# Branch A's up-projections, regrouped: head pairs of unrotated rows, one rotation product for four heads

## The reference

```python
def mla_mixer(xq, xkv, q_norm_g, w_q_up, kv_norm_g, w_kv_up):
    cq = rmsnorm(xq, q_norm_g)
    q = (cq @ w_q_up).reshape(b, s, H_A, DA_NOPE + DA_ROPE)
    q = jnp.concatenate([q[..., :DA_NOPE], rope(q[..., DA_NOPE:], pos)], axis=-1) * (DA_NOPE + DA_ROPE) ** -0.5
    ckv = rmsnorm(xkv[..., :KV_LORA], kv_norm_g)
    k_rope = rope(xkv[..., None, KV_LORA:], pos)
    kv = (ckv @ w_kv_up).reshape(b, s, H_A, DA_NOPE + DA_V)
    k = jnp.concatenate([kv[..., :DA_NOPE], jnp.broadcast_to(k_rope, (b, s, H_A, DA_ROPE))], axis=-1)
    v = kv[..., DA_NOPE:]
    ...
```

## Time and profile before

| | |
|---|---|
| median of 3 runs | 3025.38 us (3019.72 to 3032.05) |
| span of the profiled execution | 3027.5 us (the page gives no other time of it) |
| PE busy | 2832.9 us, 94% of the span |
| DVE busy | 2117.6 us, 70% |
| ACT busy | 1651.9 us, 55% |
| PE clock, mean granted | 0.972 of 2.4 GHz |
| `upA` in layer 0 | 98.24 to 127.56 us of the span |
| `upA` in layer 1 | 1590.07 to about 1619.4 us |

### The profile page before, as it was taken

One profiled execution on the slowest core, in us unless ns is written; L12 is line 12 of the kernel. 1 busy time (PEld: TensorE's weight loads), 2 busy tenths in 40 slices (PEclk: granted clock), 3 DMA queues, 4 the chain that ended last, 5 costly groups with the idle time before them and its releaser, 6 DMA issues. The chain is left out here.

```text
span 3027.5 us, 44165 instructions
## 1 busy us (share of the span) xinstructions
PE 2832.9 (94%) x14520; PEld 2263.1 (75%) x14520; DVE 2117.6 (70%) x3015; ACT 1651.9 (55%) x2612; POOL 690.0 (23%) x563
## 2 busy tenths in 40 slices
PE   5999999899899999999779999989998999999995
PEld 4677776677678888888666777866776888888884
DVE  5544456555589899999845444565546989999997
ACT  2342433432358788888534434244323778888883
POOL 0100000000145653333200000001001567533330
PEclk9999999999999999999889999999998999999997
DMA  7224342233569999999812243422334999999995
GB/s 234 79 75 148 118 134 96 74 120 133 208 239 359 354 364 373 366 373 364 309 57 80 87 153 111 153 70 90 124 120 189 349 355 353 364 381 368 369 353 228
DMA packets 124560, 671.52 MB, mean 222 GB/s; under 512 B 27628, under 2 KB 29036, under 8 KB 90444
## 3 DMA queue, kind: packets, MB, share of 16 engines
q1 hardware_dynamic: 91040, 605.91, 54.4%
q0 software_dynamic: 31424, 57.44, 5.7%
q10 hardware_dynamic: 1932, 6.16, 0.9%
HBM read 656.60 MB, written 55.28 MB: 235 GB/s over the span
## 5 line engine op out<-in xcount | busy, mean ns | idle before, releaser
L2158 DVE TENSOR_TENSOR ew_lo<-ew,e_hi 128x2048 fp32r<-128x2048 f32 x258 | 591.3, 2292 | 95.2 <-ACT e_hi L1954 95.2
L711 PE MATMUL bank<-h_hi,w_hi 128*128 128x512 f32 x1248 | 511.9, 410 | 35.1 <-DVE w_lo L645 16.5
L1954 ACT ACTIVATE e_hi<-ew 128x2048 fp32r<-128x2048 f32 x260 | 498.6, 1918 | 15.2 <-PE bank L2373 9.3
L711 PE MATMUL bank<-h_hi,w_lo 128*128 128x512 f32 x1248 | 504.3, 404 | 0.0
L711 PE MATMUL bank<-h_lo,w_hi 128*128 128x512 f32 x1248 | 502.0, 402 | 0.0
L645 DVE TENSOR_TENSOR w_lo<-raw,w_hi 128x1024 fp32r<-128x1024 f32 x198 | 242.1, 1223 | 301.1 <-ACT w_hi L637 300.6
L2373 PE MATMUL bank<-e_hi,x_hi 128*128 128x512 f32 x1040 | 418.2, 402 | 0.1
L2373 PE MATMUL bank<-ew_lo,x_hi 128*128 128x512 f32 x1040 | 408.5, 393 | 0.0
L2373 PE MATMUL bank<-e_hi,x_lo 128*128 128x512 f32 x1040 | 406.0, 390 | 0.0
L711 PEld LDWEIGHTS bank<-h_hi,w_hi 128*128 128x128 f32 x1248 | 240.1, 192 | 116.6 <-issue 44.2
L1842 POOL DMA_INDIRECT y_d<-y,idx x130 | 214.5, 1650 | 467.6 <-issue 401.0
(11 more groups left out here) (331 smaller groups left out, 5065.0 us busy)
## 6 DMA issues: line engine op xcount, KB each, us to landing
ew<-in_wexp SPq DMA_DIRECT2D x130, 2048.0 KB, 9.8
raw<-in_wmix SPq DMA_DIRECT2D x297, 512.0 KB, 3.5
ew<-in_wexp SPq DMA_DIRECT2D x130, 1024.0 KB, 10.2
ew<-y_d SPq DMA_DIRECT2D x8, 2048.0 KB, 11.7
ew<-y_d SPq DMA_DIRECT2D x8, 1024.0 KB, 7.8
ada0a<-in_ada SPq DMA_DIRECT2D x2, 2048.0 KB, 13.4
ada0b<-in_ada SPq DMA_DIRECT2D x2, 2048.0 KB, 22.2
h_d<-htok ACTq DMA_DIRECT2D x8, 512.0 KB, 10.8
```

The costliest lines, as they stand in the source:

```text
L711: ins = nc.tensor.matmul(out, lhs, rhs, start=start, stop=stop)
L1954: nc.scalar.activation(e_hi[h][:], up_part(ew, j, h), ACT.Copy).then_inc(whi_done, 1)
L2158: nc.vector.tensor_tensor(up_part(ew_lo, j, h), up_part(ew, j, h), e_hi[h][:].bitcast(F32), ALU.subtract).then_inc(wlo_done, 1)
```

## The change

It regroups `upA`. Keys: 4 jobs `knope` with two heads' 64 unrotated rows each, in place of 8. Queries: 4 jobs `qnope` with two heads' unrotated rows each and 2 jobs `qrope` with four heads' 32 rotated rows each, in place of 8 jobs of 96 rows. Values stay 4 jobs. The weights' columns are brought into that order when the tile is split (`split_parts`), since the tiles in memory stay as they were: the high and low parts are written through rearranged views. The queries go first, then key and value jobs in turn.

The copy out of a pair is two ACT instructions of 64 partitions, one for each head. The rotation is one fp32 product by a 128 x 128 matrix `turn4` for four heads, twice; DVE multiplies 128 rows twice and then adds 32 rows at a time, four times, from partitions 0, 32, 64, 96 into partitions 64 to 95 of `qA`. No rotation stands after `late`. POOL makes `turn4` from the identity at the layer's start (two operations), and SP loads the cosine and sine table four times, once for each 32 partitions.

```diff
-    j["upA"] = ([Job("T", [("kvup",)], "kA", act="ckv", k=1, col=P * h, arg=h) for h in range(HA)]
-                + [Job("VA", [("kvup",)], "vA", act="ckv", k=1, arg=t) for t in range(TC)]
-                + [Job("T", [("qup", h // 4)], "qA", act="cq", k=2, m=DQ, col=DQ * (h % 4), arg=h) for h in range(HA)])
+    j["upA"] = []
+    for t in range(2):
+        j["upA"] += [Job("T", [("qup", t)], "qrope", act="cq", k=2, col=4 * NOPE, arg=t)]
+        j["upA"] += [Job("T", [("qup", t)], "qnope", act="cq", k=2, col=P * i, arg=2 * t + i) for i in range(2)]
+    for i in range(TC):
+        j["upA"] += [Job("T", [("kvup",)], "knope", act="ckv", k=1, col=P * i, arg=i),
+                     Job("VA", [("kvup",)], "vA", act="ckv", k=1, arg=i)]
...
+        def split_parts(u, q):
+            kind = TILES[u][0]
+            src, hi, lo = raw[u % RAW][:], w_hi[q % SPLIT][:], w_lo[q % SPLIT][:]
+            if kind == "kvup":
+                src = src.rearrange("p (h a c) -> p h a c", a=2, h=HA)
+                hi, lo = [w.rearrange("p (a h c) -> p h a c", a=2, h=HA) for w in (hi, lo)]
+            if kind != "qup":
+                return [(hi, src, lo)]
+            src = src[:, 0:8 * DQ].rearrange("p (k h c) -> p k h c", k=2, h=4)
+            hi, lo = [w[:, 0:8 * DQ].rearrange("p (k c) -> p k c", k=2) for w in (hi, lo)]
+            parts = []
+            for c0, c1 in ((0, NOPE), (NOPE, DQ)):
+                h, l = [w[:, :, 4 * c0:4 * c1].rearrange("p k (h c) -> p k h c", h=4) for w in (hi, lo)]
+                parts.append((h, src[:, :, :, c0:c1], l))
+            return parts
...
-            nc.scalar.activation(w_hi[q % SPLIT][:], raw[u % RAW][:], ACT.Copy).then_inc(hi_done, 1)
+            for dst, src, _ in split_parts(u, q):
+                ins = nc.scalar.activation(dst, src, ACT.Copy)
+            ins.then_inc(hi_done, 1)
...
-            elif j.out == "kA":
-                nc.scalar.activation(kA[0:NOPE, j.arg, :], b[0:NOPE, :], ACT.Copy).then_inc(done, 1)
-            elif j.out == "qA":
-                nc.scalar.activation(qA[0:DQ, j.arg, :], b[0:DQ, :], ACT.Copy, scale=float(DQ) ** -0.5).then_inc(done, 1)
+            elif j.out in ("knope", "qnope"):
+                for i in range(2):
+                    dst = (kA if j.out == "knope" else qA)[0:NOPE, 2 * j.arg + i, :]
+                    ins = nc.scalar.activation(dst, b[NOPE * i:NOPE * i + NOPE, :], ACT.Copy,
+                                               scale=1.0 if j.out == "knope" else float(DQ) ** -0.5)
+                ins.then_inc(done, 1)
+            elif j.out == "qrope":
+                nc.scalar.activation(qrope[j.arg][:], b[:], ACT.Copy, scale=float(DQ) ** -0.5).then_inc(done, 1)
...
-                    sp.dma_start(rope_t[R, :, :], rope_d).then_inc(rope_in, 16)
+                    for i in range(4):
+                        sp.dma_start(rope_t[ROPE * i:ROPE * i + ROPE, :, :], rope_d).then_inc(rope_in, 16)
...
+                        nc.vector.tensor_tensor(qrot[:], MB[:], rope_t[:, 1, :], ALU.mult).then_inc(m_free, 1)
+                        link(dve, nc.vector.tensor_tensor(qrope[t][:], qrope[t][:], rope_t[:, 0, :], ALU.mult))
+                        for i in range(4):
+                            rows = slice(ROPE * i, ROPE * i + ROPE)
+                            nc.vector.tensor_tensor(qA[R, 4 * t + i, :], qrope[t][rows, :], qrot[rows, :], ALU.add
+                                                    ).then_inc(rot_ready, 1)
                     for j in jobs["upA"]:
                         dve_stream(dve, events_of([(j, 0, n_products(j))]))
-                        if j.out == "qA" and j.arg:
-                            rotate(j.arg - 1)
+                        if j.out == "qnope" and j.arg % 2 == 0:
+                            rotate(j.arg // 2)
                     dve_stream(dve, events_of(whole(jobs["late"])))
-                    rotate(HA - 1)
...
+                        nc.tensor.matmul(MB[:], turn4[:], qrope[t][:], start=True, stop=True).then_inc(m_full, 1)
```

More of the change, by code:

```diff
@@ L260, in hybrid_trunk @@
         lamv = place("lamv", [P, 256], at=m0 + 10240)
+        qrope = [place(f"qrope{i}", [P, S], at=m0 + 11264 + 2048 * i) for i in range(2)]
+        turn4 = place("turn4", [P, P], at=m0 + 15360)
+        assert t_end["turn4"] <= t_end["merged"]
         r0 = cursor[0]
@@ L382, in hybrid_trunk @@
         vecs_in, rope_in = sem("vecs_in"), sem("rope_in")
[L383 removed]
+        made_ready = sem("made_ready")
         amul_ready = sem("amul_ready")
@@ L581, in hybrid_trunk @@
         for key in ([("st", n) for n in ("x",)] + [("rb", "x"), ("rb", "cq"), ("rb", "ckv"), ("kr", 0)]
-                    + [("qr", h) for h in range(HA)] + [("ot", o) for o in range(16)] + [("st", "x2"), ("rb", "x2")]):
+                    + [("qr", t) for t in range(2)] + [("ot", o) for o in range(16)] + [("st", "x2"), ("rb", "x2")]):
             m_use[key] = len(m_use)
@@ L679, in make_products @@
                 for i, (w, a) in enumerate(parts):
-                    wv = W[w][:, 0, :].rearrange("p (h c) -> p h c", h=HA)[:, :, NOPE:]
-                    out.append((u, 0, A[a][:, 0, j.arg * P:(j.arg + 1) * P], wv, bank[:].rearrange("p (h c) -> p h c", h=HA),
+                    out.append((u, 0, A[a][:, 0, j.arg * P:(j.arg + 1) * P], W[w][:, 0, HA * NOPE:], bank[:],
                                 i == 0, i == 2))
@@ L724, in act_out @@
             done = chunk_out[j.c % 2]
-            if j.out not in ("cq", "ckv", "kA", "qA", "qB", "kB", "qC", "kC", "qD", "kD", "gate", "sg", "vt"):
+            if j.out not in ("cq", "ckv", "knope", "qnope", "qrope", "qB", "kB", "qC", "kC", "qD", "kD", "gate", "sg", "vt"):
                 return
@@ L1333, in _ @@
                     pool.wait_ge(pchain, 1)
-                    nc.gpsimd.memset(tabA[0:64, S - 64:S], NEG).then_inc(tabA_ready, 1)
+                    nc.gpsimd.memset(tabA[0:64, S - 64:S], NEG).then_inc(made_ready, 1)
+                    four = [P, 4, ROPE // 2]
+                    heads, eye = [a.rearrange("p (h c) -> p h c", h=4) for a in (turn4[:], ident)]
+                    nc.gpsimd.tensor_tensor(heads[:, :, 0:ROPE // 2], zero[:, 0:1].unsqueeze(2).broadcast_to(four),
+                                            eye[:, :, ROPE // 2:], ALU.subtract).then_inc(made_ready, 1)
+                    nc.gpsimd.tensor_copy(heads[:, :, ROPE // 2:], eye[:, :, 0:ROPE // 2]).then_inc(made_ready, 1)
                     load_table(0)
@@ L1492, in _, with rotate @@
                     nc.tensor.matmul(MB[R, :], prot, qraw[R, :], start=True, stop=True).then_inc(m_full, 1)
-                    def rotate(h):
-                        wait_out_of(pe, "qA", h)
-                        wait_mb_free(pe, ("qr", h))
-                        nc.tensor.matmul(MB[R, :], prot, qA[R, h, :], start=True, stop=True).then_inc(m_full, 1)
+                    def rotate(t):
+                        wait_out_of(pe, "qrope", t)
+                        pe.wait_ge(made_ready, 3)
+                        wait_mb_free(pe, ("qr", t))
+                        nc.tensor.matmul(MB[:], turn4[:], qrope[t][:], start=True, stop=True).then_inc(m_full, 1)
                     for j in jobs["upA"]:
                         pe_products(pe, j, 0, n_products(j))
-                        if j.out == "qA" and j.arg:
-                            rotate(j.arg - 1)
+                        if j.out == "qnope" and j.arg % 2 == 0:
+                            rotate(j.arg // 2)
                     products_of(jobs["late"])
-                    rotate(HA - 1)
                     for br in "ABCD":
```

22 lines of the change are left out of this document (10 added, 12 removed).

## The result

The changed kernel takes 3009.21 us (median of 4 runs, 3005.16 to 3012.63) where the kernel before, on the same chip, takes 3025.36 (4 runs): a ratio of 0.9941, 95% interval 0.9927 to 0.9954. So it is 16.2 us faster, inside the range of the prediction (2996 to 3014), but 6 us short of its 3003, and at the upper edge of the 2998 to 3009 that it gave the forecast itself. The profiled execution took 3010.46 us, with a span of 3008.8 against 3027.5.

The account below looks back on a forecast made before the run. PE bounds the query part, the bank's round the key/value part, and a rotation and bias wait follow `late`. Per layer 8.2 + 1.06 + 1.64 = 10.9 us, twice 21.8, from 3025.38: 3003 us, range 2996 to 3014.

Parts of the forecast that it names:

- Priced at nothing: Side effects given no cost: SP's three more table loads, POOL's two operations, its copies of rotated key rows, tile loads.
- its walk: Job-by-job schedule from the first up product: queries 10.7 us, keys and values 10.4, `late` at 21.1 instead of 29.32.
- The four additions: DVE's additions in the new query rotation: 0.71 us each, bounded at 1.36, within 4.16 us for the whole rotation.
- The splits of the query tiles: Weight splits in two instructions, priced as before at 1.06 us on ACT and 1.22 on DVE, bounded at twice.
- The gain behind `late`: No last rotation behind `late`, 1.06 us on PE, and second scores sooner after the first, 1.64 us, per layer.
- the 128 x 128 rotation: PE's product rotating four heads of queries: 1.16 us with its gap, as the old rotation, bounded at 1.4.
- The 12 products taken out here are worth nothing: Key/value part: 10.4 us against 10.13 before; the double copy and its queue take back what fewer products give.
- The clock's: Rival: gaps in the key part lower PE's clock, `late` pays up to 5.5 us per layer: 3014 us, chance 0.10.
- Dear rearranging: Rival: DVE additions at 1.36 us and double splits cut the gain to 4.5 to 5.7 per layer: 3015 us, chance 0.10.
- layer 0's loads: Rival: three held table loads delay tile 3 to 75.9, costing up to 7 us once: 3010 us, chance 0.06.
- Nothing gained: Rival: PE's lead is given back by a later stage that waits for something else: 3025 us, chance 0.04.
- slower: Rival: lasting half clock from the key part through `late` into branch A's first steps: 3035 us, chance 0.03.

Follow-up runs that it names:

- changed, second profile: The changed kernel unaltered, run again beside its variants: 3008.09 us against 3029.31 of before, ratio 0.9931.
- POOL's copy later: Changed kernel with POOL's copy of the rotated key rows moved behind DVE's low split of the late tile: 3006.44 us, ratio 0.9930 to before.
- POOL's copy beside the rotation: Changed kernel with POOL's copy started by the event that starts DVE's first query rotation: 3009.43 us in one run, beside 3031.26.
- old keys: Changed kernel with the key/value part as before, queries new and first, POOL's copy where it was: 3005.31 us, ratio 0.9922 to before.
- old keys, POOL's copy later: Changed kernel with the key/value part as before and POOL's copy behind the late tile's low split: 3007.59 us, ratio 0.9930 to before.
- before, split in two halves: Kernel before with DVE's low split of the first query tile in two plain halves: 3030.87 us in one run, beside 3029.31 of before.
- new keys alone: Kernel before with only the key/value part changed, keys first and old queries: 3026.71 us beside 3027.69 of before, ratio 0.9999.
- reordered: Changed kernel with POOL's copy started at the first key pair and ACT's and DVE's queues reordered, no shared copies: 3001.56 us, ratio 0.9908 to before.
- reordered, shared copies: The reordered kernel with each key pair copied half by ACT and half by DVE: 2998.74 us, ratio 0.9910 to before.
- experiment 7: Changed kernel with POOL's copy and ACT's and DVE's queues moved, without and with key-pair copies shared by ACT and DVE: 3001.56 and 2998.74 us.

## Why the prediction was right, and where it fell short

The stretch from the first up-projection product to `late`, in us, by kernel (layer 0, layer 1), each from first starts of its timeline:

| kernel | layer 0 | layer 1 |
|---|---|---|
| before | 29.32 | 29.36 |
| forecast for the changed one | 21.1 | 21.1 |
| changed, first profile | 24.82 | 22.88 |
| changed, second profile | 22.87 | 22.87 |
| POOL's copy later | 20.93 | 20.91 |
| POOL's copy beside the rotation | 24.87 | 23.08 |
| old keys | 22.98 | 22.99 |
| old keys, POOL's copy later | 21.98 | 22.01 |
| before, split in two halves | 29.32 | 29.32 |
| new keys alone | 28.71 | 28.65 |
| reordered | 19.96 | 19.97 |
| reordered, shared copies | 19.22 | 19.22 |

**The step that failed** stands under "Priced at nothing": "The copies of the rotated key rows on POOL end long before the first scores." That is true, and answers the wrong question. It asks who waits for POOL, and not whom POOL holds. The change cuts the split beside it in two, the second piece comes up behind the copy's start, and 1.0 us of work lasts 4.0. Of those 3 us, 1.3 show in the query part (11.84 against 10.55) and 0.65 in the key part (11.03 against 10.38), where DVE's queue is late: 1.95 us per layer. With that hold gone, the forecast's parts are 10.55 for 10.7 and 10.38 for 10.4, and its stretch 20.92 for 21.1. The steps of its walk are there too: in the kernel with POOL's copy later, ACT's copies of the four key pairs start at 113.97, 116.22, 118.47 and 120.73 us, the first 12.9 us behind the first up product (forecast 13.0) and then in rounds of 2.25 us, as priced.

**Terms that held.** A pair's two copies take 1.20 us. The four additions take 2.83, DVE's whole rotation 4.19 (in the changed kernel the first starts at 107.13, what follows at 111.32) for 4.16, although the rows move between partitions. (Two thirds of 2.03 are 1.35 and not the 1.32 that the prediction took for the multiplications; measured were 1.32, 107.13 to 108.45.) The splits of the query tiles take 0.93 us on ACT and 1.03 on DVE, the rearranged one of the key tile 1.23. The gain behind `late` is 9.15 - 6.46 = 2.7 us per layer, as summed. **A term mis-sized, in the kernel's favour:** the 128 x 128 rotation costs PE 0.86 us and not 1.16. In the kernel with POOL's copy later, the product before it starts at 103.73 and the second one after it at 105.05, 1.32 us less two products of 0.23; it is not dearer than the product on 32 rows that it replaces. The query part was only 0.15 us under its price all the same: a product costs 0.233 us and not 0.23, and PE's weight loads stood still twice for ACT's copies, 0.33 us at 107.66 and 0.34 at 109.23, where one short wait was priced.

**A reading that was too strong:** "The 12 products taken out here are worth nothing." It compared the new part in its new place with the old part in its old place. Like for like the new key part, with its fewer products, double copies and new order together, is worth 0.7 us in the old place, 1.1 in the new with POOL out of the way, and 0.1 with POOL in the way; never near 2.8. The mechanism given for it, that the bank's round and not PE's work sets the pace, is what experiment 7 confirmed: with PE's work unchanged, other queues and copies took 1.7 us off this part.

**The sum.** 6.45 us (29.32 to 22.87) and 2.69 make 9.1 per layer where 10.9 was forecast: 18.3 us in all. The two comparisons gave 16.2 and 21.2; that the second is so near the 21.8 of the forecast is chance. The prediction gave 0.75 to a gain beyond half a per cent; the interval of the first comparison, 0.9927 to 0.9954, just fails to exclude less than that, and that of the second, 0.9914 to 0.9948, excludes it. The first profile had the fall of the clock on top, 1.95 us in layer 0. Its span is 18.7 us shorter; the parts changed give 7.2 us in layer 0 and 9.1 in layer 1, 16.3 together. What is left over lies in stretches that the change does not touch: the first up product comes 2.6 us later, the way from `late` to layer 1's part is 5.7 us shorter than the 2.7 explain, and the rest behind layer 1's `late` 0.8 longer. What moves them was not traced. From `late` to layer 1's part, the eight profiles of kernels with the new queries took between 1450.1 and 1460.4 us.

**The rivals.** The clock's came, but in one of the four layers profiled of the changed program, and it cost 1.95 us where 5.5 were priced, since it was back to 0.96 by the time of `late`. A fall in the key part is also one of the signs by which the prediction calls itself wrong. Its waits there, priced at 0.5 to 1.2 us, reached 2.02. The kernel with the copy beside the rotation fell in layer 0 as well (24.87 against 23.08). Both executions had also had the fall at 74 to 86 us and came to this part at 100.9 us; two kernels with as much of the early fall, but without the 2 us waits in the key part, kept 1.00; and the changed kernel's second profile had such a wait (2.00 us), no early fall, and kept 1.00. That suggests that the waits matter, but not alone; what decides it stays open. The rule of the Trainium skill's page TensorE: Matmul & The Clock Gate, section "A second HAM failure mode", is borne out in layer 0 and not in the others. Dear rearranging did not come, nor did layer 0's loads: SP was held 17.02 us by the four table loads instead of 4.54, but in none of the traces did a weight load of PE between 60 and 90 us wait for a DMA. With the clock at 1.00 from 74 to 86 us in both, the changed kernel reached its first up product at 97.01 us and the kernel before, in the version with two halves, at 97.41. Nothing gained and slower did not come.

## What to carry to other kernels

Before an instruction is cut in two, or moved, look at what POOL does at that time: an instruction of DVE with two SBUF inputs that used to slip in ahead of a POOL copy can, cut in two, leave its second piece to wait, and the profile books the wait as busy. A long POOL copy belongs beside DVE instructions that have at most one input in SBUF: those met here, which read PSUM, were free of it. And where two banks go round, taking products out can be worth little until the copies and the queue in front of them are dealt with: here moves in the queues and a shared copy gave 1.7 us per layer, more than the regrouped key part with its twelve products fewer did (1.1).

## What the runs showed of the hardware

- The hold goes both ways. POOL's copy of 32 x 3584 takes 3.17 us where nothing opposes it, 3.69 where a DVE split of 0.69 us has begun 0.04 us before it, and 4.23 where one of 1.23 us has begun 0.03 us before it. The excess, 0.52 and 1.06 us, is 0.13 and 0.14 us short of what was left of the split.
- Three forms of DVE instruction met that copy: both inputs in SBUF, held to about its end (3.21 us at the rotation, 3.39 in the changed kernel, 3.66 for the second plain half); one in PSUM and one in SBUF, free (0.69); a copy out of PSUM, free (0.69).
- A DVE copy of 64 partitions of PSUM to the other 64 of SBUF takes 0.69 us, as much as one of 128 partitions in place.
- The same program had its granted clock at 0.72 in one execution and at 1.00 in another from 80 to 86 us, with PE dense in both, and reached the changed part 3.8 us apart, this and a slower start together. A difference of a few us between two spans says nothing until the clock of the stretches between is compared.
- That early fall follows the column sums in front of it by their time, not by the kernel. Over the eleven profiles the clock fell behind them where they began at 74.21 and 74.56 us and at 75.58 to 75.78 (four profiles), and stayed at 1.00 in the five where they began at 74.76 to 75.37. Nothing was run to test this.
